# One product of 56 columns for the narrow projections, and first chunks without the zero state

## The reference, cut to what matters

```python
def token_mixing(x, w_in, ...):
    h = x @ w_in
    h_rw, h_gla, h_gdn, h_gate = _split(h, GROUP_SPLITS)
    # h_rw: 1536 columns r, k, v, then 288 columns of low-rank inputs (64 + 64 + 160)
    # h_gla: q, k, v, then 16 columns gk_lo, then the gate;  h_gdn: 1536 columns q, k, v, then 4 + 4 columns a, b, then the gate
    ...

def gla_mix(...):                       # a scan over chunks of 64 tokens
    def step(S, inp):
        o = att @ v_c + (q_c * exp(b_c)) @ S
        S = S * exp(b_end)[..., None] + (k_c * exp(b_end - b_c)).T @ v_c
        return S, o
    S0 = zeros

def gated_deltanet_mix(...):            # the same kind of scan
    def step(S, inp):
        v_new = u_c - w_c @ S
        o = (q_c * exp(g_c)) @ S + att_c @ v_new
        S = S * exp(g_end) + (k_c * exp(g_end - g_c)).T @ v_new
        return S, o
    S0 = zeros
```

## Time and profile before

| | before |
|---|---|
| median of 3 runs | 3308.22 us (3306.82 to 3317.57) |
| profiled execution | 3308.98 us, span 3306.9 us |
| TensorE busy | 3097.9 us, 21806 matmul records |
| VectorE busy | 1792.9 us |
| ScalarE busy | 700.5 us |
| share of the 16 DMA engines, weight queue | 36.8% |
| granted TensorE clock, mean | 0.975 |

### The profile page before, as it was taken

One profiled execution on the slowest core, in us unless ns is written; L12 is line 12 of the kernel. 1 busy time (PEld: TensorE's weight loads), 2 busy tenths in 40 slices (PEclk: granted clock), 3 DMA queues, 4 the chain that ended last, 5 costly groups with the idle time before them and its releaser, 6 DMA issues. The chain is left out here.

```text
span 3306.9 us, 50880 instructions
## 1 busy us (share of the span) xinstructions
PE 3097.9 (94%) x21806; PEld 2405.8 (73%) x21806; DVE 1792.9 (54%) x2682; ACT 700.5 (21%) x1330; POOL 37.9 (1%) x76
## 2 busy tenths in 40 slices
PE   8999988999998999998899998988999999998998
PEld 8987774558985998675466995554888885555797
DVE  5554555556554564454565564674343562287565
ACT  1112213212112101212312113271111012144110
POOL 1000000000000100000000000000000000000000
PEclk9999999999999999999999999999999999998999
DMA  8644402226645755322214743110232442221452
GB/s 275 230 166 150 165 28 77 77 77 220 205 163 186 246 191 200 112 82 71 84 52 151 261 166 133 60 40 26 77 102 77 140 159 89 102 102 58 135 172 102
DMA packets 279695, 430.75 MB, mean 130 GB/s; under 512 B 9880, under 2 KB 147456, under 8 KB 279472
## 3 DMA queue, kind: packets, MB, share of 16 engines
q1 hardware_dynamic: 273920, 411.52, 36.8%
q0 software_dynamic: 5088, 14.86, 1.4%
q10 hardware_dynamic: 464, 1.12, 0.1%
HBM read 426.43 MB, written 1.05 MB: 129 GB/s over the span
## 5 line engine op out<-in xcount | busy, mean ns | idle before, releaser
L452 PE MATMUL bank<-xT,ring 128*128 128x128 f32 (+3 forms) x4640 | 805.6, 334 | 20.0 <-ACTq L2824 9.9
L452 PE MATMUL bank<-arena 128*128 128x128 f32 (+8 forms) x7196 | 764.2, 284 | 53.0 <-DVEq L3690 8.9
L452 PEld LDWEIGHTS bank<-xT,ring 128*128 128x128 f32 (+1 forms) x4640 | 689.9, 194 | 129.5 <-issue 55.0
L452 PEld LDWEIGHTS bank<-arena 128*128 128x128 f32 (+3 forms) x7196 | 662.0, 164 | 154.6 <-issue 27.1
L452 PE MATMUL bank<-ring,xT 128*128 128x512 f32 (+2 forms) x1408 | 590.8, 571 | 16.9 <-ACT xT L2816 8.8
L452 PEld LDWEIGHTS bank<-ring,xT 128*128 128x128 f32 x1408 | 260.4, 194 | 286.8 <-issue 267.9
L452 PE MATMUL bank<-ring,arena 128*128 128x256 f32 (+1 forms) x1584 | 447.6, 435 | 19.7 <-DVE arena L845 6.5
L452 PEld LDWEIGHTS bank<-ring,arena 128*128 128x128 f32 x1584 | 302.3, 193 | 139.0 <-issue 90.0
L788 DVE TENSOR_TENSOR arena<-arena,bank 128x256 f32<-128x256 f32 (+1 forms) x198 | 92.2, 466 | 426.5 <-PE bank L452 287.0
L700 ACT COPY arena<-bank 128x256 f32<-128x256 f32 (+1 forms) x264 | 107.6, 408 | 777.2 <-PE bank L452 776.2
L748 DVE TENSOR_TENSOR arena<-ring,arena 128x1024 f32<-128x1024 f32 (+1 forms) x216 | 257.1, 1190 | 7.4
(11 more groups left out here) (387 smaller groups left out, 2123.5 us busy)
## 6 DMA issues: line engine op xcount, KB each, us to landing
ring<-in_ffn_w SPq DMA_DIRECT2D x88, 1024.0 KB, 7.9
ring<-in_w_in SPq DMA_DIRECT2D x32, 2048.0 KB, 7.7
ring<-in_ffn_w_in SPq DMA_DIRECT2D x44, 1024.0 KB, 6.6
arena<-in_ada_w SPq DMA_DIRECT2D x18, 2048.0 KB, 13.3
ring<-in_ffn_w SPq DMA_DIRECT2D x16, 2048.0 KB, 7.9
ring<-in_ffn_w_out SPq DMA_DIRECT2D x12, 2048.0 KB, 7.9
ring<-in_hgrn_w_in SPq DMA_DIRECT2D x12, 2048.0 KB, 7.9
ring<-in_ffn_w SPq DMA_DIRECT2D x8, 1536.0 KB, 6.6
```

The source lines that it names most:

```text
L452: return self.e.matmul(o, lhsT, rhs, start=start, stop=stop, skip_group_check=True)
```

## The change

The 24 narrow columns are loaded beside the 288 low-rank ones and multiplied in the same tile: its last tile has 56 columns in place of 32. Their results lie on partitions 32 to 55 of that tile's bank. VectorE copies these (24 partitions, 256 tokens) to `gla_lo`; `gk2`, which is multiplied with the first 16 of them, moves to partitions 32 to 47. The 8 columns that are wanted with tokens on partitions come out of `gla_lo` by two transposes of 24 rows, and one ScalarE copy in place of two.

In the first chunk of each mixer the products with the state are left out, since the state is zero; what was an addition to them becomes a plain copy. The states are no longer set to zero. In the gated delta rule VectorE copies the values to `dX` without waiting for TensorE; it waits for ScalarE's cleared tiles (`own_rows_clear`) instead.

```diff
-                wide(W[l], 1536, 288)
+                load((0, 0, k_rows(W[l], 1536, 288)), (0, 288, k_rows(W[l], GLA0 + 1024, 16)),
+                     (0, 304, k_rows(W[l], GDN0 + 1536, 8)))
...
-                load((0, 0, k_rows(W[l], GLA0 + 1024, 16)), (0, 16, k_rows(W[l], GDN0 + 1536, 8)))
...
-        gk2 = lnp[0:16, 1, 512:768]
+        gk2 = lnp[32:48, 1, 512:768]
+        NARROW = slice(32, 56)
...
-            blk = pe.block()
-            pe_T(pe, blk, to_dve, 0, [P, P, 32])
+            blk = pe.block(3)
+            pe_T(pe, blk, to_dve, 0, [P, P, NARROW.stop])
...
-            blk = pe.block(2)
-            pe_T(pe, blk, to_act, 0, [16])
-            pe_tok(pe, blk, to_act, 16, 8, x_lhs)
-            pe.used()
+            pe.wait_ge(to_act.freed, to_act.next_free())
+            bank = to_act.free_bank()
+            for tt in range(2):
+                mm = pe.e.transpose(bank[:, 24 * tt:24 * tt + 24], gla_lo[NARROW, tt * P:(tt + 1) * P], ident[NARROW, NARROW])
+            mm.then_inc(to_act.filled, 1)
...
-            act.e.copy(gla_lo[0:16, :], bank[0:16, 0:SEQ]).then_inc(to_act.freed, act.up(to_act.freed))
+            act.e.copy(gdn_ab[:], bank[:, 0:48].rearrange("p (t n) -> p t n", t=2)[:, :, 16:24]
+                       ).then_inc(to_act.freed, act.up(to_act.freed))
...
+                if gi == 1:
+                    v.tensor_copy(gla_lo[NARROW], bank[NARROW, 0:SEQ]).then_inc(dve_step, dve.up(dve_step))
+                    dve.wait_ge(dve_step, dve.sent(dve_step))
...
-            v.memset(Hst[:], 0.0).then_inc(dve_step, dve.up(dve_step))
-            dve.wait_ge(dve_step, dve.sent(dve_step))
             dve.sem_inc(v_tok_ready, dve.up(v_tok_ready))
-            dve.sem_inc(state_ready, dve.up(state_ready))
...
+                    if tt == c == 0:
+                        v.tensor_tensor(Hst[:], added, decay, ALU.mult).then_inc(to_dve.freed, dve.up(to_dve.freed))
...
-                        pe.mm(o, AR[:, par, hp, ct], Hst[:, hp], True, False)
-                        mm = pe.mm(o, M4[:, h, 0], v_own[tt][c][:, h * 64:(h + 1) * 64], False, True)
+                        if tt or c:
+                            pe.mm(o, AR[:, par, hp, ct], Hst[:, hp], True, False)
+                        mm = pe.mm(o, M4[:, h, 0], v_own[tt][c][:, h * 64:(h + 1) * 64], tt == c == 0, True)
...
-                        pe.mm(o, AR[:, 2 + par, hp, ct], Hst[:, hp], True, False)
+                        if tt or c:
+                            pe.mm(o, AR[:, 2 + par, hp, ct], Hst[:, hp], True, False)
...
-            v.memset(gS[:], 0.0).then_inc(dve_step, dve.up(dve_step))
...
-                    for hp in range(2):
+                    if tt == c == 0:
+                        ins = v.tensor_copy(gS[:], bank[:, 0:2 * P].rearrange("p (a n) -> p a n", a=2))
...
-                        mm = pe.mm(o, gQb[:, par, o0:o0 + 64], gS[:, hp], False, True)
+                        if tt or c:
+                            mm = pe.mm(o, gQb[:, par, o0:o0 + 64], gS[:, hp], False, True)
...
-            v.memset(dSt[:], 0.0).then_inc(dve_step, dve.up(dve_step))
...
+                    if first:
+                        dve.wait_ge(own_rows_clear, dve.due(own_rows_clear, 2))
+                        v.tensor_copy(dX[c][r_], dv_tok[r_, tt]).then_inc(dve_step, dve.up(dve_step))
...
-                    pe.wait_ge(state_ready, pe.due(state_ready))
-                    for t0 in (4, 0):
+                    if tt or c:
+                        pe.wait_ge(state_ready, pe.due(state_ready))
+                    for t0 in (4, 0) if tt or c else ():
```

More of the change, by code:

```diff
@@ L1425, in act_mix @@
                 act.wait_ge(to_act.freed, act.sent(to_act.freed))
+            act.sem_inc(gla_in_ready, act.up(gla_in_ready))
             act.wait_ge(to_act.filled, to_act.next_filled())
             bank = to_act.filled_bank()
-            act.e.copy(gla_lo[0:16, :], bank[0:16, 0:SEQ]).then_inc(to_act.freed, act.up(to_act.freed))
+            act.e.copy(gdn_ab[:], bank[:, 0:48].rearrange("p (t n) -> p t n", t=2)[:, :, 16:24]
+                       ).then_inc(to_act.freed, act.up(to_act.freed))
             act.wait_ge(to_act.freed, act.sent(to_act.freed))
[L1430 to L1435, removed]
             act.wait_ge(rwkv_T_ready, act.due(rwkv_T_ready))
@@ L2416, in dve_gdn @@
                     r_ = slice(64 * c, 64 * c + 64)
-                    dve.wait_ge(to_dve.filled, to_dve.next_filled())
-                    bank = to_dve.filled_bank()
-                    for h in range(4):
+                    first = tt == c == 0
+                    if first:
+                        dve.wait_ge(own_rows_clear, dve.due(own_rows_clear, 2))
+                        v.tensor_copy(dX[c][r_], dv_tok[r_, tt]).then_inc(dve_step, dve.up(dve_step))
+                        dve.wait_ge(dve_step, dve.sent(dve_step))
+                    else:
+                        dve.wait_ge(to_dve.filled, to_dve.next_filled())
+                        bank = to_dve.filled_bank()
+                    for h in () if first else range(4):
                         s_ = slice(h * P, (h + 1) * P)
@@ L2434, in dve_gdn @@
                     y3 = br_tok[r_, tt].rearrange("p (h n) -> p h n", h=4)
[L2435 to L2440, removed]
+                    if not first:
+                        dve.wait_ge(to_dve.filled, to_dve.next_filled())
+                        bank = to_dve.filled_bank()
+                        v.tensor_tensor(y3, bank[r_, :].rearrange("p (h n) -> p h n", h=4),
+                                        eG_s[r_, 4 * tt:4 * tt + 4].unsqueeze(2).broadcast_to([64, 4, P]),
+                                        ALU.mult).then_inc(to_dve.freed, dve.up(to_dve.freed))
+                        dve.wait_ge(to_dve.freed, dve.sent(to_dve.freed))
                     dve.wait_ge(to_dve.filled, to_dve.next_filled())
@@ L2464, in dve_gdn @@
                     bank = to_dve.filled_bank()
-                    for h in range(4):
+                    if first:
+                        ins = v.tensor_copy(dSt[:], bank[:].rearrange("p (h n) -> p h n", h=4))
+                        ins.then_inc(to_dve.freed, dve.up(to_dve.freed))
+                        dve.wait_ge(to_dve.freed, dve.sent(to_dve.freed))
+                    for h in () if first else range(4):
                         o = (4 * tt + h) * 2 + c
```

36 lines of the change are left out of this document (22 added, 14 removed).

## The result

| | before | after |
|---|---|---|
| median, runs taken side by side | 3307.52 us (4 runs, 3302.41 to 3317.57) | 3278.82 us (4 runs, 3274.61 to 3280.23) |
| ratio after to before | | 0.9908, 95% interval 0.989 to 0.9926 |
| profiled execution | 3308.98 us, span 3306.9 us | 3274.61 us, span 3272.8 us |

A forecast was written before the change was run, and what follows sets the result against it. TensorE, busy for 94% of the span, was taken as the bound. Terms of 12.06 us a layer gave 24.1 us for two layers, 27.4 with the clock's 3.3, so 3308.98 became 3281.6 us, range 3271 to 3293.

The forecast's parts named there:

- The narrow products: 24-column block joins the first block's last tile at no cost for width, two transposes added: 6.8 us gained a layer.
- VectorE's copy: Added 24x256 copy before the second shift-mixing group: nothing on the path, 0.4 us if its cover were gone.
- The loads: Two small parts added to the first block's load, one load dropped: cost 0, within 4.3 us of slack.
- The memset: RWKV state memset ahead of the signal TensorE waits for: 0 to 0.3 us gained a layer, 0.15 taken.
- RWKV: First chunk, zero-state records dropped from first product and readout: 2.0 us gained a layer.
- GLA: First chunk, eight readout records dropped and two state additions become one copy: 1.25 us gained a layer (0.9 to 1.4).
- gated delta rule: First chunk, 16 zero-state records dropped, only the gate step left before the solved product: 1.86 us gained a layer.
- The clock: Second layer's narrow stretch: the granted clock's fall inside the 8-column products goes with them, 3.3 us more gained.
- B: Clock takes some back as everything behind the first mixer shifts and chunks lose dense work: 3287 to 3296 us; chance 0.22.
- D: First block's small loads are late, deciding beyond 4.3 us behind the big part; chance 0.02.
- C: Other waits replace the first chunks' products, only the narrow products count: 13.6 us gained, 3295 us; chance 0.05.
- E: Clock stays low through the thinned chunk chains: 30 us lost against 24.1 gained, 3315 us; chance 0.02.

The follow-up runs named there:

- own block: Kernel before with the 24 columns kept as their own block, all stationary, two transposes replacing the 8-column products: 3295.49 us, ratio 0.9961.
- the ten copies: Changed kernel with VectorE's copy of the 24 rows done ten times, the RWKV memset put back and the delta rule's values copied four times: 3279.24 us.
- the run with twelve more: Changed kernel with twelve further small parts of 64 and 32 KB in the first block's load, into unread columns: 3301.6 us, one execution.
- four passes: Kernel before with the 8-column products of the narrow block done four times: 3351.07 us, ratio 1.013.
- the narrow half: Kernel before with only the 24 columns moved into the 56-column tile, zero-state products kept: 3288.75 us, ratio 0.9933.
- the zero-state half: Kernel before with only the first chunks' zero-state products and the state memsets removed, narrow block as before: 3292.46 us, ratio 0.9948.
- dense four times: Kernel before with the 16-column product of the narrow block done four times: 3326.17 us, ratio 1.0057.

## Why the prediction was right

- **What bounds the kernel** was read rightly: TensorE's busy time fell by 33.9 us and the span by 34.1 (some 10 of it the clock's), and in front of the narrow stretch, where it had no idle time, each removed record was worth its duration.
- **The narrow products**: 6.8 us a layer forecast, 6.90 measured. The width of the stationary side costs nothing: the 16 records of the 56-column tile take 3.66 us, beside 3.63 for 16 stationary columns, as the prediction named it for a sign. Two transposes of 24 rows cost 0.23 us, below my 0.33 and just under the lower bound of 0.25, and with the own block they start at 396.10 and the next product at 396.24, 0.14 us.
- **VectorE's copy** at 0: right, shown by the ten copies.
- **The loads** at 0: right in the sum, with wrong working. I let the small parts land wholly behind the big one, in 2.8 us. They land 5.3 to 5.7 us after their own issue, beside it, and some 3 us before they are wanted. What would use up the slack is their issue, 1.06 us from one to the next in the run with twelve more, and then the last one's landing. The Trainium skill (DMA: Bandwidth & Descriptors, opening table) speaks of pieces under 512 bytes as missing line rate. The run with twelve more agrees: from 247 to 251 us, with almost only such pieces to move, the DMA engines are busy for a share of 0.65 and move 48 GB/s, and from 257 to 262 us, with full rows, 1.00 and 367 GB/s. In the change itself it costs nothing.
- **The memset**: 0.15 forecast, 0.29 measured, and 0.28 when put back. I took the middle of 0 and 0.3; the upper end held.
- **RWKV** 2.0 forecast, 1.88 measured; **GLA** 1.25 and 1.18; **gated delta rule** 1.86 and 2.01, the further 0.15 us in hand-overs later in the chunk. The three covers named at 0 (the state's addition in RWKV, the copy of the values, the state's copy in the delta rule) show no idle time in after.
- **The sum**: 24.1 us forecast, 24.5 measured. Its ends were added up wrongly: the low and high ends named term by term give 2 x (6.49 + 0 + 2.0 + 0.9 + 1.7) = 22.2 us and 2 x (6.90 + 0.3 + 2.0 + 1.4 + 1.86) = 24.9 us, not 21.4 and 26.6, since RWKV has no ends of its own. The measured sum lies inside either pair.
- **The clock**: 3.3 us forecast from one low stretch. The mechanism was right: that stretch went, and gave just its 3.3 us. The size was not: it stood in one layer of one execution, while one pass costs 2.7 us in each layer on average, 5.4 us in all (4.0 to 9.6). And it is not the whole of the clock's part: the profiled pair gained some 10 us, of which this stretch is a third. The rule of the Trainium skill that was weighed there (TensorE: Matmul & The Clock Gate, "Why this matters for your kernels") ties a fallen clock to idle gaps; four passes with TensorE shown busy throughout ran at 0.50, so the measurement goes beyond the rule, though the waits of the run with more loads, at 0.50 too, agree with it.
- **The whole**: 24.5 + 5.4 = 29.9 us, and the change was measured at 28.7 and at 31.1 us. The same sum gives 13.8 + 5.4 = 19.2 for the narrow half (19.0 measured) and 6.8 + 5.4 = 12.2 for the own block (12.5). For the whole the fit is partly luck: it leaves no room for the 4.6 us that the zero-state half gave beyond its records, and with them the sum is 34.5. Nor is the forecast of 27.4 us shown to be short: it lies within both intervals, 24.5 to 36.4 and 27.1 to 39.0 us.
- **The rivals**: B, the clock taking some back, did not come; D's transfers were not late in the change, and the run with twelve more showed what late costs; C's chains did not hide the gain (the zero-state half alone is worth 15.3 us); E did not come, since the mean clock rose.

What stays open: the zero-state half gives 15.3 us where its records give 10.7, with the 8-column products kept. By its interval (11.2 to 23.5 us) at least 0.5 us of the difference of 4.6 is real. Its one profile has no dip at the 8-column products of either layer, and a higher clock over the RWKV chunks; either could be what gives the time, and nothing here tells them apart or ties them to the edit. So a shift can still have a share in the change's time, though not the one that the products have. That dense four times came out at 18.2 us for 21.4 is within its interval.

## What to carry to other kernels

Look in front of a narrow product on its own: a tile with free stationary columns takes it in at no cost, and transposes bring out the part that is wanted the other way round. Cost an edit record by record from its own stretch, say for each step what covers it, and when the clock's share matters, price it by kernels of equal length (dense records in the place of thin ones), not by a low stretch in one profile. For loads in small pieces, count the row of their issues and then the landing of the last one.

## What the runs showed of the hardware

- Products that stream 8 columns behind 128x128 weight loads can lower the granted clock although TensorE is shown busy: 0.50 for three windows of 7 us at four passes, 1.00 with dense records in the same place; 25 us between the two kernels for equal time of records at full clock. After one pass it dips in four of eight cases.
- DMAs of 64 and 32 KB in 64- and 32-byte pieces, fourteen in a row, hold the issuing queue 0.58 to 2.73 us apiece, 1.06 us from one to the next, where a block of full rows takes 0.37 us on a free queue and took 1.57 us right behind them.
- Two float32 transposes of 24 rows and 128 tokens delay TensorE's next product by 0.14 us (own block) to 0.23 us (the change).
